# Refilling the first expert rooms row by row and ending the last columns in two steps, in a two-layer float32 forward pass

## The reference

```python
logits = einsum('bld,de->ble', u, w_router)
aff = softmax(logits)
g, idx = top_k(aff.transpose(0, 2, 1), cap)          # cap = 2 * 256 / 16 = 32
xin = u[idx]                                          # 32 tokens of each expert
hg, hu = xin @ w_gate, xin @ w_up                     # 1024 x 1024 of each expert
eo = (silu(hg) * hu) @ w_down
x = x + scatter_add(idx, eo * g)
```

## Time and profile before

| | us |
|---|---|
| median of 3 runs | 1196.56 (1194.89 to 1196.99) |
| the profiled execution, its own time | 1196.45 |
| its span, first to last instruction | 1194.5 |
| PE busy | 1098.5 (92%) |
| DVE busy | 507.0 (42%) |
| ACT busy | 419.2 (35%) |
| moved by DMA | 309.45 MB, mean 259 GB/s |

### The profile page before, as it was taken

How to read it: one execution, slowest core, us unless ns; L and a number is a source line. 1 busy time by engine, 2 the same in 40 slices (tenths; PEclk the granted TensorE clock), 3 DMA queues, 4 the chain that set the end, 5 groups by cost and what they waited for, 6 DMA issues and landing times.

```text
span 1194.5 us, 16626 instructions
## 1 busy us (share of the span) xinstructions
PE 1098.5 (92%) x6691; PEld 785.0 (66%) x6691; DVE 507.0 (42%) x999; ACT 419.2 (35%) x800; POOL 16.4 (1%) x28
## 2 busy tenths in 40 slices
PE   7999999999999999999999996998978797879786
PEld 6988988888999999798678885332323232323231
DVE  4778774795666555676875323010101000100011
ACT  4667666844666444664345312000100000000000
POOL 3000000000000000000000000000000000000000
PEclk9999999999999999999999997999999999999998
DMA  8735334343465667254241985799999999999995
GB/s 230 247 116 190 116 130 145 128 157 135 148 211 157 176 163 208 83 199 141 72 141 72 361 333 221 295 427 427 428 427 427 429 427 428 427 428 430 424 422 235
DMA packets 95108, 309.45 MB, mean 259 GB/s; under 512 B 6016, under 2 KB 41096, under 8 KB 83080
## 3 DMA queue, kind: packets, MB, share of 16 engines
q1 hardware_dynamic: 94296, 307.42, 66.8%
q0 software_dynamic: 496, 1.07, 0.4%
q10 hardware_dynamic: 256, 0.10, 0.0%
HBM read 307.53 MB, written 1.05 MB: 258 GB/s over the span
## 4 chain that ended last, share of the span: by engine, by line
PE 72%; DMA 23%; DVE 3%; ACT 1%; issue 1%; SPq 1%; ACTq 0%; DVEq 0%
PE bank L438 71%; DMA parts_room<-in_w_up 7%; DMA arena<-in_w_down 4%; DMA parts_room<-in_w_down 3%; DMA arena<-in_w_up 3%; DMA ring<-in_w_down 3%; DMA xh<-in_w_down 2%; SPq L1137 1%; PE bank L671 0%; DMA arena<-in_x 0%; DVE parts L1689 0%; DVE roots_room L1661 0%; DVE hidden_parts L1901 0%; DVE arena L2218 0%; ACT parts L1262 0%
## 5 line engine op out<-in xcount | busy, mean ns | idle before, releaser
L438 PE MATMUL bank<-parts 128*128 128x256 f32 (+1 forms) x2352 | 299.8, 288 | 1.4 <-issue 1.2
L438 PEld LDWEIGHTS bank<-parts 128*128 128x128 f32 x2352 | 288.3, 191 | 15.2 <-issue 12.0
L1262 ACT ACTIVATE parts<-ring 128x512 fp32r<-128x512 f32 x328 | 203.7, 629 | 227.1 <-PE bank L438 218.2
L1689 DVE TENSOR_TENSOR parts<-ring,parts 128x512 fp32r<-128x512 f32 x328 | 218.9, 689 | 120.5 <-ACT parts L1262 118.7
L438 PE MATMUL bank<-hidden_parts,parts 128*128 128x256 f32 x1024 | 164.9, 283 | 0.0
L438 PE MATMUL bank<-arena 128*32 128x512 f32 (+4 forms) x548 | 149.7, 487 | 11.3 <-DMA arena<-in_w_down 2.7
L438 PE MATMUL bank<-arena,roots_room 128*32 128x512 f32 x400 | 131.6, 607 | 15.4 <-DMA ring<-in_w_gate 5.5
L438 PEld LDWEIGHTS bank<-hidden_parts,parts 128*128 128x128 f32 x1024 | 141.4, 192 | 0.1
L2205 DVE TENSOR_TENSOR sqr<-bank,arena 128x512 f32<-128x512 f32 x8 | 5.2, 686 | 273.5 <-ACT arena L1579 273.5
L438 PEld LDWEIGHTS bank<-arena 128*128 128x128 f32 (+2 forms) x548 | 78.8, 194 | 54.1 <-issue 40.8
L438 PE MATMUL bank<-ring,roots_room 128*32 128x512 f32 x224 | 98.2, 600 | 7.8 <-DMA xh<-in_w_up 4.0
(11 more groups left out here) (300 smaller groups left out, 955.3 us busy)
## 6 DMA issues: line engine op xcount, KB each, us to landing
ring<-in_w_in SPq DMA_DIRECT2D x21, 2048.0 KB, 8.0
arena<-in_w_gate SPq DMA_DIRECT2D x14, 2048.0 KB, 34.6
arena<-in_w_down SPq DMA_DIRECT2D x13, 2048.0 KB, 37.1
arena<-in_w_up SPq DMA_DIRECT2D x11, 2048.0 KB, 36.8
ring<-in_w_ff_in SPq DMA_DIRECT2D x8, 2048.0 KB, 7.8
ring<-in_w_ff_out SPq DMA_DIRECT2D x8, 2048.0 KB, 9.0
parts_room<-in_w_up SPq DMA_DIRECT2D x8, 2048.0 KB, 36.8
ring<-in_w_gate SPq DMA_DIRECT2D x7, 2048.0 KB, 35.3
```

The lines of the kernel that those rows point to most:

```text
L438: return nc.tensor.matmul(o, lhsT=l, rhs=r, start=first, stop=last)
L1262: A(w_part[0][:, p % PIECES], piece_of(n, p), ACT.Copy).then_inc(S("pieces rounded"), 1)
L1689: X.tensor_tensor(w_part[1][:, p % PIECES], piece_of(n, p), w_part[0][:, p % PIECES].bitcast(F32), ALU.subtract).then_inc(S("pieces split" ...
```

## The change

What it does:

- First attention: `att_scores` waits for the two padded copies of its own key head, not for all eight. `pad_keys(3)` stands ahead of `round_half(EARLY)` on ACT. On DVE, `rest_of_half(7)` stands ahead of the last two of the eight selection rounds and of `key_bias(0)`.
- First gather: slices 0 and 1 into bank 6, slices 2 and 3 into bank 5, each scaled by DVE when it is there.
- First q-step: all four experts row by row (8 products each), a semaphore after every row. SP refills the four rooms (units 10 to 13) row by row: after each row four loads of 512 KB, 4 KB in one piece per partition; 16 loads in place of 4. PE waits for all of them before it reads units 10 to 13.
- Last q-step: eight loads of 1 MB in place of four of 2 MB, 2 KB in one piece: the four rows of the lower 512 columns, then the four of the upper. PE finishes the lower half, ACT copies it and PE scatters it before the upper pieces are taken. ACT makes both copies to `eo`, in all groups; the lower one as soon as its 512 columns are summed.

```diff
@@ PE, first attention
-                pe.wait_ge(S("keys padded"), 8)
+                pe.wait_ge(S("keys padded"), 2 * g + 2)
@@ PE, first gather
-            take(6, ("gathered", 6))
-            gather(6, slice(0, P))
+            for b, first in ((6, 0), (5, 2)):
+                take(b, ("gathered", b))
+                for k in range(2):
+                    for t in range(TT):
+                        last = mm(bank[b][:, k * P:k * P + P], un[:, t, spaced(first + k)], pick[:, t, 0:P], t == 0, t == 1)
+                last.then_inc(S("gathered" if b == 6 else "rest gathered"), 1)
@@ PE, unit_ready
+                    if n in by_rows:                      # range(10, 14)
+                        pe.wait_ge(S("rows refilled"), 16 * len(by_rows) * (RUN - 1))
@@ PE, first q-step
-                block(0, (0, 1), 0, xg, 0)
-                block(0, (2, 3), 0, xg, 0)
+                def first_block_by_rows():
+                    for e in range(GROUP):
+                        unit_ready(e)
+                    for j in range(RUN):
+                        if j == 2:
+                            wait_taken(("gathered", 5))
+                        for h in range(2):
+                            last = product(0, range(GROUP), 0, xg, 0, h, j)
+                        if j < RUN - 1:
+                            last.then_inc(S("expert row"), 1)
+                        else:
+                            last.then_inc(S("expert block"), GROUP // PAIR)
@@ PE, end of the last group
+                def last_pieces(h):
+                    for j in range(RUN):
+                        n = LAST_ROWS + (RUN * h + j) // 2
+                        if h == 1 and j == 2:
+                            pe.wait_ge(S("last piece but one loaded"), 16)
+                        else:
+                            pe.wait_ge(moe_loaded[n % MOE_RING], 16 * (n // MOE_RING + (1 if h and j == 3 else 2)))
+                        for e in range(GROUP):
+                            last = mm(bank[4 + h][CAP * e:CAP * e + CAP, :],
+                                      hhT[:, KD - RUN + j, CAP * e:CAP * e + CAP], last_piece(RUN * h + j)[:, e, :],
+                                      False, j == RUN - 1)
...
                 for h in range(2):
+                    if last_group:
+                        last_pieces(h)
                     pe.wait_ge(emptied[4 + h], g * (3 - h) + (ug[4 + h] + 3 - h))
@@ SP, at unit 10 (units 10 to 13)
+            def refill_by_rows():
+                for j in range(RUN):
+                    if j < RUN - 1:
+                        sp.wait_ge(S("expert row"), j + 1)
+                    else:
+                        sp.wait_ge(S("expert block"), GROUP // PAIR)
+                    for n in by_rows:
...
+                        sp.dma_start(moe_slot(n)[:, 0, j, :], rows_of[:, j, :])\
+                            .then_inc(S("rows refilled") if j < RUN - 1 else moe_loaded[n % MOE_RING], 16)
@@ SP, units 92 to 95
+                    for i in (2 * (n - LAST_ROWS), 2 * (n - LAST_ROWS) + 1):
+                        h, j = i // RUN, i % RUN
+                        sp.dma_start(last_piece(i), rows_of[:, j, :, 512 * h:512 * h + 512])\
+                            .then_inc(S("last piece but one loaded") if i == 2 * RUN - 2 else moe_loaded[n % MOE_RING], 16)
@@ ACT
-            round_half(EARLY)
             pad_keys(3)
+            round_half(EARLY)
...
+                act.wait_ge(S("lower half summed"), g + 1)
+                A(eo[:, 0:512], bank[4][:, :], ACT.Copy).then_inc(emptied[4], 1)
                 act.wait_ge(S("expert block"), g * BLOCKS + BLOCKS)
-                A(eo[:, 0:512], bank[4][:, :], ACT.Copy).then_inc(emptied[4], 1)
+                A(eo[:, 512:1024], bank[5][:, :], ACT.Copy).then_inc(emptied[5], 1)
@@ DVE
-            select_rounds(0, range(0, 8))
+            select_rounds(0, range(0, 6))
+            rest_of_half(7)
+            select_rounds(0, range(6, 8))
             key_bias(0)
-            rest_of_half(7)
...
-            dve.wait_ge(S("gathered"), 1)
-            take_gathered()
+            for b, first in ((6, 0), (5, 2)):
+                dve.wait_ge(S("gathered" if b == 6 else "rest gathered"), 1)
+                for k in range(2):
+                    ins = X.tensor_scalar(xg[:, first + k, :], bank[b][:, k * P:k * P + P], ...)
+                empty(ins, ("gathered", b))
...
-                dve.wait_ge(S("expert block"), g * BLOCKS + BLOCKS)
-                X.tensor_copy(eo[:, 512:1024], bank[5][:, :]).then_inc(emptied[5], 1)
```

More of the change, by code:

```diff
@@ L345, in two_layers, with last_piece @@
         moe_loaded = [S(f"expert ring slot {s} loaded") for s in range(MOE_RING)]
+        by_rows = range(MOE_RING, MOE_RING + GROUP)
+        def last_piece(i):
+            room = moe_room[(LAST_ROWS + i // 2) % MOE_RING]
+            return room[:, UNIT // 2 * (i % 2):UNIT // 2 * (i % 2 + 1)].rearrange("p (e c) -> p e c", c=512)
         def moe_slot(n):
@@ L995, in experts, with product, block @@
                     pe.wait_ge(emptied[b], g * 2 + ug[b])
-                def block(u, pair, banks, src, q):
+                def product(u, pair, banks, src, q, h, j):
+                    k = RUN * q + j
+                    for e in pair:
+                        w = moe_slot(first_unit + u + e)[:, 0, j, 512 * h:512 * h + 512]
+                        last = mm(bank[banks + h][CAP * e:CAP * e + CAP, :], src[:, k, CAP * e:CAP * e + CAP], w,
+                                  k == 0, k == KD - 1)
+                    return last
+                def block(u, pair, banks, src, q, lower=""):
                     for i in pair:
@@ L1001, in block @@
                         for j in range(RUN):
[L1002 to L1006, removed]
-                    last.then_inc(S("expert block"), 1)
-                block(0, (0, 1), 0, xg, 0)
-                block(0, (2, 3), 0, xg, 0)
+                            last = product(u, pair, banks, src, q, h, j)
+                        if h == 0 and lower:
+                            last.then_inc(S(lower), 1)
+                    last.then_inc(S("expert block"), 1)
+                def first_block_by_rows():
[10 more added lines that the diff above has]
+                            last.then_inc(S("expert block"), GROUP // PAIR)
+                if g:
+                    block(0, (0, 1), 0, xg, 0)
+                    block(0, (2, 3), 0, xg, 0)
+                else:
+                    first_block_by_rows()
                 pe.wait_ge(emptied[7], g + ug[7])
@@ L1038, in experts @@
                     if not (last_group and q):
-                        for pair in ((0, 1), (2, 3)):
-                            block(2 * KD + RUN * q, pair, 4, hhT, q)
-                if last_group:
+                        block(2 * KD + RUN * q, (0, 1), 4, hhT, q)
+                        block(2 * KD + RUN * q, (2, 3), 4, hhT, q, "lower half summed" if q else "")
+                def last_pieces(h):
                     for j in range(RUN):
[L1043 to L1050, removed]
+                        n = LAST_ROWS + (RUN * h + j) // 2
[7 more added lines that the diff above has]
+                                      False, j == RUN - 1)
+                        if j == RUN - 1:
+                            last.then_inc(S("expert block" if h else "lower half summed"), 1)
+                        elif h == 0 and j == 1:
                             last.then_inc(S("expert block"), 1)
                 for h in range(2):
+                    if last_group:
+                        last_pieces(h)
                     pe.wait_ge(emptied[4 + h], g * (3 - h) + (ug[4 + h] + 3 - h))
@@ L1130, in _ @@
                 first = g * GROUP + some * (u % RUN)
+                if n in by_rows:
+                    if n == by_rows[0]:
+                        refill_by_rows()
+                    continue
                 if n < MOE_RING:
@@ L1338, in _ @@
             half(5, 0)
+            pad_keys(3)
             round_half(EARLY)
-            pad_keys(3)
             half(5, 1)
@@ L2191, in _ @@
             dve.wait_ge(S("expert norm loaded"), 16)
-            dve.wait_ge(S("gathered"), 1)
-            take_gathered()
+            for b, first in ((6, 0), (5, 2)):
+                dve.wait_ge(S("gathered" if b == 6 else "rest gathered"), 1)
+                for k in range(2):
+                    ins = X.tensor_scalar(xg[:, first + k, :], bank[b][:, k * P:k * P + P], expert_norm[:, first + k:first + k + 1],
+                                          None, ALU.mult)
+                empty(ins, ("gathered", b))
             choose(GROUP, EXPERTS)
```

5 lines of the change are left out of this document (3 added, 2 removed).

## The result

The changed kernel takes 1184.49 us (median of 4 runs, 1184.15 to 1184.61) against 1195.72 for the kernel before on the same chip: a ratio of 0.9907, 95% interval 0.9893 to 0.9921, so 11.2 us faster. The profiled execution took 1184.61 us. Its span is 1182.65, against 1194.53 before: 11.9 less. Forecast were 1186.7 and a range of 1182.8 to 1191.5.

What follows compares the result with a forecast made beforehand. PE was taken to bound the kernel until about 740 us, the load stream from the first refill on. First attention -1.9, start -6.5, rate +1.9 and end -3.3 gave -9.8 us: 1186.7, range 1182.8 to 1191.5.

Steps and rivals of the forecast that it cites:

- Three regions: PE bounds until about 740 us, the load stream from the first refill on, with a hole in DMA between.
- First attention, -1.9: First attention: 0.3 of a 0.65 us PE stall and all of a 1.60 us stall on padded copies saved.
- The start, -6.5: Gather to first refill: refill issued at 748.0 us after one row of 3.4 us, not at 754.55.
- bounds of -8.2 and -5: Start of stream: -8.2 with the clock up before the row (1.9 us), -5 if four-wide products were as slow as two-wide.
- That the stream stays full: After the first refill: four rooms last to about 769 us, the third block ends about 765, some 4 us reserve.
- The rate, +1.9: Load stream: smaller packets cost +0.9 us on refilled rows and +1.0 on the last pieces at 390 GB/s.
- A dip under 400 GB/s between the last pieces: Sign that the forecast is wrong, in the load stream's last pieces; also named for 750 to 775 us.
- the rival that it gave: Queued small loads run well under large ones: 1190.2 us at 369 GB/s, 1194.1 at 340; chance 0.11.
- The end, -3.3: After the last landing: half the last piece's products saves 1.6 us, two of four scatter products 1.7.
- bounds of -2.6 and -5.7: End: -2.6 if PE picks up slower after a wait, -5.7 if denser small pieces hold the clock at 1.00.
- The sum: Whole kernel: -1.9 - 6.5 + 1.9 - 3.3 = -9.8 us, so 1186.7.
- the second rival: Clock up earlier at the start and the end: -1.7 and -2.4 us more, 1182.6; chance 0.15 for both.

Runs made afterwards that it cites:

- the kernel before kept busy there: Kernel before, with three products on constant data into an unused bank ahead of each of the last two units: 1193.79 us, ratio 0.9990.
- blocks: Changed kernel with the first q-step in two blocks of two experts, units 10 to 13 refilled whole, two-bank gather kept: 1190.56 us, ratio 0.9953.
- whole units: Changed kernel, first q-step still row by row for four experts, but units 10 to 13 loaded whole after the fourth row: 1190.42 us, ratio 0.9956.
- busy start: Changed kernel with three products on constant data into an unused bank while PE waits for the ranks of the tokens: 1184.11 us, ratio 0.9907.
- small loads: Changed kernel with units 14 to 91 also loaded as four loads of 512 KB in packets of 4 KB: 1202.44 us, ratio 1.0065.

## Why the prediction was right

**What bounds.** Three regions, as put: the PE region passes its gain on unchanged (633.1 to 633.2 us from first attention to gather in every trace), the stream is full from the first refill to the last landing, and only its start, rate and end count.

**First attention, -1.9.** Measured -1.95. Of its parts, the 0.65 us wait comes back as 0.46 one half later, where the text took 0.3 of it as gain; the order is worth 0.1. The padded keys and ACT's order bring the other 1.85, where 1.6 was put.

**The start, -6.5.** Measured -7.6, within the bounds of -8.2 and -5. The mechanism was right; the term that was mis-sized is the first row, put at 3.4 us for the half clock of the earlier trace rows. It took 2.4 us (743.74 to 746.1): there is no idle 1.3 us between gather and products any more, and the clock came up during the row; that was named as the bound. The gather ends and the first product starts at 4.00 us, as put. That the stream stays full holds: DMA's share is 1.03 from 750 to 770 us, and PE has no wait for a load between 745 and 800 us. The recorded bounds do not quite follow from their terms: a row at 1.9 us gives -8.0, and 16 steps of 0.43 us make 6.9 us and so -3.0, not -5; the measured value lies between them either way. What was not foreseen is how little the side-by-side products matter by themselves: with units loaded whole, 5.2 of the 5.9 us are lost, and the other 0.7 comes from starting before DVE has scaled the second pair.

**The rate, +1.9.** Measured +2.0: 0.6 or 1.1 for the refilled rows (from the two runs that load them whole; put at 0.9) and 1.2 for the last pieces (put at 1.0, from 390 GB/s). In the trace after, nine microseconds of those pieces read:

```profile
DMA packets 1753, 3.48 MB, mean 387 GB/s; under 512 B 53, under 2 KB 53, under 8 KB 1753
```

A dip under 400 GB/s between the last pieces had been named as a sign of being wrong, though the sum itself put them at 390: the sign was set too high. SP is stuck in the last issues for up to 17.7 us, and nothing comes of it.

The Trainium skill, DMA: Bandwidth & Descriptors, asks under Rules for kernel authors for at least 1 MiB in each load, and the 341 GB/s for 1 MB in its table under Bandwidth gave the prediction's estimate of +9 us; that table is of loads issued from GpSimd, not of a queue that SyncE keeps full. The sum by that figure would have been -2.6, not near nothing. No run here bears it out for a full queue: loads of 512 KB keep 409 GB/s. The measurement decides; the rival that it gave falls with it.

**The end, -3.3.** Measured -5.5, within the bounds of -2.6 and -5.7 (whose lower term adds up to -6.0). At the full clock half the products are worth 0.9 (1.97 for 1.11) and half the scatters 1.7 (3.71 for 2.00), 2.5 in all by the ends (9.6 for 7.0); the rest, 2.9, is the clock, which fell in the last unit of the earlier trace rows and did not in the profiled execution after. The text had put the products at 1.6, half of what they took mostly at half clock, and left the clock as it was. The text took ScalarE's second copy for nothing; the run with VectorE's copy shows that without it the end would have won 1.2 us less, with the work that stood behind that wait. In the trace of the kernel before kept busy there the end is 2.9 us shorter with no other change. The denser pieces do not secure this: in four of the traces with the new end (blocks, whole units, busy start, small loads) the clock fell all the same and the end took 8.5 to 9.6 us.

**The sum.** -9.8 was put and -11.2 measured between medians. The terms come to -13.0 in the traces; the startup, 1.1 us later ahead of all that the change touches, hides a part. So the closeness of the number is partly luck. In the profiled execution the second rival, the clock up earlier in both places, had most of its way: -1.1 of its -1.7 at the start and -2.2 of its -2.4 at the end. It had been given 0.15. The last landing, 1175.62 us in the profile, had been put near 1175.5, by the same compensation: the startup against the faster first row.

## What to carry to other kernels

When a load stream is the bound, look for the stretch where the queue is empty because no room is free, and order the consumer so that it gives back a slice of every room at once and the loader refills slices; consuming side by side without refilling by slices brought almost nothing here. Products added only to keep PE busy stand in front of real ones: at the end here they cost 1.0 us. In a full queue a load may be as small as the 512 KB tried here as long as its packets are not: price it by the packet, 428, 410 and 387 GB/s for 16, 4 and 2 KB here (the last in loads of 1 MB). At the end of such a stream, split the work by output columns rather than by the summed dimension, so that half of the tail is done before the last byte lands.

## What the runs showed that was not expected

- A gather of sixteen 128x128 records takes 4.07 us at a granted clock of 0.50 and 3.97 at 1.00; PE's weight loads are busy for 3.8 to 3.9 us of it.
- An idle stretch of 1.29 us on PE between the gather and the products goes with a clock that comes up 8.1 to 8.9 us after the gather's start instead of 3.8 to 5.5 (in three traces against eight), and the trace without it reaches the first refill 2.25 us earlier, not 1.36. Where the clock was up before the idle began, nothing of this showed.
- Products added to keep PE busy at the end held up the last real ones by 1.0 us.
- One copy on the engine that also adds, in front of the additions in its order, went with an end 1.2 us longer; the difference in the copy's duration is 0.1.
- The clock at the start (up at 11.8 to 15.0 us) and at the end (which came 7.0 to 9.6 us after the last landing) differs between executions of nearly the same program; it makes 1.6 and 2.6 us. Effects under 1 us had to be read from stretches of the trace.
